# Turning angles moved from VectorE to GpSimd, with new orders on ScalarE and VectorE at five places

## The reference, cut to what matters

```python
def s5_ssm(u, a_re, a_im, log_dt, b_re, b_im, c_re, c_im, d_skip, glu_w, glu_b):
    lam = lax.complex(a_re, a_im)
    lam_bar = jnp.exp(lam * jnp.exp(log_dt)[:, None])
    b_bar = ((lam_bar - 1.0) / lam)[..., None] * b_mat
    bu = jnp.einsum('bsgh,gph->bsgp', ug, b_bar)
    _, states = lax.associative_scan(combine, (a_seq, bu), axis=1)
    y = jnp.real(jnp.einsum('bsgp,ghp->bsgh', states, c_mat))
...
def first_block(x, ...):
    for layer in range(DEPTH):
        h = rmsnorm(x, pre_norm[layer])
        y = even_mixer(h, ...) if layer % 2 == 0 else odd_mixer(h, ...)
        x = x + rmsnorm(y, post_norm[layer])
...
def second_block(x, ...):
    for layer in range(DEPTH):
        h = h + hybrid_mixer(rms_norm(h, norm1_g[layer]), ...)
        h = h + expert_choice_ffn(rms_norm(h, norm2_g[layer]), ...)
    return rms_norm(h, final_norm_g)
```

## Time and profile before

| | us |
|---|---|
| median of 3 runs | 1636.35 |
| lowest and highest | 1635.52, 1637.13 |
| profiled execution, own time | 1636.07 |
| its span in the trace | 1634.2 |

### The profile page before, as it was taken

How to read it: one execution, slowest core, us unless ns; L and a number is a source line. 1 busy time by engine, 2 the same in 40 slices (tenths; PEclk the granted TensorE clock), 3 DMA queues, 4 the chain that set the end, 5 groups by cost and what they waited for, 6 DMA issues and landing times.

```text
span 1634.2 us, 28359 instructions
## 1 busy us (share of the span) xinstructions
PE 1307.5 (80%) x12516; PEld 923.0 (56%) x12516; DVE 574.0 (35%) x873; ACT 453.5 (28%) x580; POOL 137.4 (8%) x169
## 2 busy tenths in 40 slices
PE   8999999999999987566666667999987556565665
PEld 6789889998989743223222234889843223232232
DVE  7993774765484520000000001584521001000001
ACT  5337654445554311001010012555311001010011
POOL 0220200000314000000000000304000000000000
PEclk9999999999999999988899897999999988899878
DMA  8334344545435899999999999335899999999997
GB/s 279 104 129 155 117 172 155 200 163 204 155 139 197 371 426 426 428 428 428 428 429 428 429 428 405 139 113 222 344 427 427 427 429 429 428 428 428 429 426 301
DMA packets 79503, 515.59 MB, mean 316 GB/s; under 512 B 6544, under 2 KB 6928, under 8 KB 54592
## 3 DMA queue, kind: packets, MB, share of 16 engines
q1 hardware_dynamic: 76000, 509.21, 76.4%
q0 software_dynamic: 912, 2.83, 0.5%
q10 hardware_dynamic: 2512, 2.36, 0.4%
HBM read 513.33 MB, written 1.05 MB: 315 GB/s over the span
## 4 chain that ended last, share of the span: by engine, by line
DMA 45%; PE 38%; DVE 11%; ACT 2%; issue 2%; SPq 1%; DVEq 0%; ACTq 0%
DMA board<-in_w_down 24%; DMA board<-in_w_gate 21%; PE dense L1750 8%; PE dense L1752 8%; PE dense L1751 8%; PE bank L2321 4%; PE bank L2351 2%; DVE ring_parts L1273 2%; DMA ring<-in_even_w_in 1%; DVE board L1556 1%; ACT ring_parts L883 1%; DVE board L1547 1%; PE dense L1773 1%; PE bank L2144 1%; PE bank L2291 1%
## 5 line engine op out<-in xcount | busy, mean ns | idle before, releaser
L2321 PE MATMUL bank<-ring,board 128*32 128x256 f32 x2688 | 207.4, 459 | 145.7 <-DMA ring<-in_w_up 82.5
L2321 PEld LDWEIGHTS bank<-ring,board 128*32 128x32 f32 x2688 | 90.4, 124 | 257.1 <-DMA ring<-in_w_up 104.2
L1107 ACT ACTIVATE board<-bank 128x256 f32<-128x256 f32 x32 | 12.3, 384 | 731.7 <-PE bank L2321 731.7
L1273 DVE TENSOR_TENSOR ring_parts<-ring,ring_parts 128x4096 fp32r<-128x4096 f32 (+1 forms) x43 | 181.6, 4228 | 88.6 <-ACT ring_parts L883 88.5
L1663 DVE TENSOR_TENSOR board<-board,bank 128x256 f32<-128x256 f32 x32 | 13.5, 421 | 553.3 <-ACT board L1107 553.3
L883 ACT ACTIVATE ring_parts<-ring 128x4096 fp32r<-128x4096 f32 (+1 forms) x47 | 161.5, 3438 | 123.7 <-DMA ring<-in_w_in 31.7
L1750 PE MATMUL dense<-board_parts,ring_parts 128*128 128x256 f32 x624 | 179.4, 288 | 0.5 <-DVE ring_parts L1273 0.5
L1752 PE MATMUL dense<-board_parts,ring_parts 128*128 128x256 f32 x624 | 176.6, 283 | 0.0
L2321 PE MATMUL bank<-board 128*32 128x256 f32 x1408 | 108.8, 461 | 65.4 <-DMA board<-in_w_up 40.7
L1750 PEld LDWEIGHTS dense<-board_parts,ring_parts 128*128 128x128 f32 x624 | 119.7, 192 | 1.9 <-issue 1.6
L1752 PEld LDWEIGHTS dense<-board_parts,ring_parts 128*128 128x128 f32 x624 | 119.6, 192 | 0.0
(11 more groups left out here) (354 smaller groups left out, 2057.3 us busy)
## 6 DMA issues: line engine op xcount, KB each, us to landing
ring<-in_w_gate SPq DMA_DIRECT2D x44, 2048.0 KB, 41.4
ring<-in_w_up SPq DMA_DIRECT2D x40, 2048.0 KB, 41.6
ring<-in_w_down SPq DMA_DIRECT2D x40, 2048.0 KB, 41.0
board<-in_w_up SPq DMA_DIRECT2D x24, 2048.0 KB, 41.0
board<-in_w_gate SPq DMA_DIRECT2D x20, 2048.0 KB, 40.5
board<-in_w_down SPq DMA_DIRECT2D x20, 2048.0 KB, 40.7
ring<-in_w_in SPq DMA_DIRECT2D x18, 2048.0 KB, 7.8
ring<-in_even_w_in SPq DMA_DIRECT2D x9, 2048.0 KB, 8.6
```

The lines of the kernel that those rows point to most:

```text
L1273: tt(lo, slot_of(u), hi.bitcast(F32), ALU.subtract).then_inc(lo_done, 1)
L2321: last = mm(o.rearrange("p (m b) -> p m b", b=2), xeT[:, 4 * (j // 2) + k, :], cols.rearrange("p (m r b) -> p r m b", r=2, b=2)[:, q % 2], ...
```

## The change

1. The angles of the state space part are made by GpSimd, in five instructions instead of VectorE's eight, behind the transfer of the C matrix and ahead of the turning of the queries; the rounding of sine and cosine is done in one instruction of 2048 columns each. `frac_ready` counts to 1 instead of 2. The two roundings' memory is a free piece of the working area.
2. ScalarE makes unit 2's high part behind the copy of unit 0's result (L899) instead of ahead of it and of three DMA issues.
3. VectorE makes the low parts of units 1 and 2 between the products and the differences of a round of B's powers. Each stood behind a round's differences before, and now has the next round's two products ahead of it as well.
4. Seam 1: VectorE's addition of the second tile goes ahead of the first tile's gain differences; the quarters of unit 15's low part go behind the second tile's gain.
5. Seam 2: one quarter of the low part of the second unit moves from ahead of the second tile's normalising to behind its gain.
6. At both ends of the experts ScalarE sums the squares of a tile by halves (`rms_halves`), the first as soon as its half of x is there.

```diff
@@ GpSimd
             gp.wait_ge(rest_in, 16)
+            gp.wait_ge(phi_ready, 1)
+            nearest = area(14336, "p (f n) -> p f n", f=2, n=SSM_TILES * SB)
+            own.link(g.tensor_tensor(cs[:, 1, :].rearrange("p (t b) -> p t b", t=SSM_TILES),
+                                     cn("block_start").unsqueeze(1).to_broadcast([P, SSM_TILES, SB]),
+                                     small[:, 0, :].unsqueeze(2).to_broadcast([P, SSM_TILES, SB]), ALU.mult))
+            own.link(g.tensor_scalar(cs[:, 0, :], cs[:, 1, :], 0.25, None, ALU.add))
+            own.link(g.tensor_scalar(nearest, cs, ROUND, None, ALU.add))
+            own.link(g.tensor_scalar(nearest, nearest, -ROUND, None, ALU.add))
+            g.tensor_tensor(cs, cs, nearest, ALU.subtract).then_inc(frac_ready, 1)
...
@@ ScalarE
             high_part(1)
-            high_part(2)
             act.dma_start(masks[:].rearrange("p l n -> p (l n)"), a["pair_masks"]).then_inc(masks_in, 16)
...
             act.wait_ge(unit_done, 1)
             s.activation(u_steps, DP[0][:].rearrange("p z (c b i) -> p (z c) i b", c=2, i=SL), ACT.Copy).then_inc(dense_out, 1)
+            high_part(2)
...
                 load_sqrt()
                 for i in range(NT):
-                    act.wait_ge(x_ready, 6 + 6 * l + 2 * (i + 1))
-                    rms(i, x[:, i, :])
+                    at = 6 + 6 * l + 2 * i
+                    rms_halves(i, x[:, i, :].rearrange("p (b n) -> p b n", b=2), (x_ready, at + 1), (x_ready, at + 2))
...
@@ VectorE
             for i in reversed(range(SL)):
                 times(z, sm(3), sm(4))
+                if i in (1, 2):
+                    low_part(3 - i)
                 z = pair(B_AT + 32 * i)
                 own.go(tt(z[:, 0], by_re[:, 0], by_im[:, 1], ALU.subtract))
                 own.link(tt(z[:, 1], by_re[:, 1], by_im[:, 0], ALU.add))
-                if i >= 2:
-                    low_part(4 - i)
...
             dve.wait_ge(rest_in, 16)
-            own.link(tt(turns(1), cn("block_start").unsqueeze(1).to_broadcast([P, SSM_TILES, SB]),
-                        sm(0).unsqueeze(2).to_broadcast([P, SSM_TILES, SB]), ALU.mult))
-            own.go(ts(cs[:, 0, :], cs[:, 1, :], 0.25, None, ALU.add))
...
-            tt(cs[:, 0, :], cs[:, 0, :], nearest[0], ALU.subtract).then_inc(frac_ready, 1)
...
@@ VectorE, seam 1
+            def norm_between(name):
+
+                dve.wait_ge(row_in, 16)
+                add_rows(0, 1)
...
+                normalise(0)
+                gain_rows(0, name)
+                add_rows(1, 1)
+                gain_low(0, x_lo)
...
+                normalise(1)
+                gain_rows(1, name)
+                low_part(SECOND[0], 0)
+                gain_low(1, x_lo)
+                for n in range(1, 4):
+                    low_part(SECOND[0], n)
...
@@ VectorE, seam 2
                 add_rows(i, 2)
-                for n in range(2):
+                for n in range(1 if i else 2):
                     low_part(FIRST2[0] + i, n)
...
-                gain_out(i, "n1_0", x_lo2)
-            for n in range(2, 4):
+                gain_rows(i, "n1_0")
+                gain_low(i, x_lo2)
+            for n in range(1, 4):
                 low_part(FIRST2[0] + 1, n)
```

More of the change, by code:

```diff
@@ L838, in sincos @@
             def sincos(c):
-                act.wait_ge(frac_ready, 2)
+                act.wait_ge(frac_ready, 1)
                 angle = cs[:, :, 4 * SB * c:4 * SB * (c + 1)]
@@ L1139, in normalise, with gain_out @@
                     ts(xs[:, i, half], x[:, i, half], rstd[:, i:i + 1], None, ALU.mult).then_inc(xs_ready, 1)
-            def gain_out(i, name, low=None):
+            def gain_out(i, name):
                 for half in range(2):
@@ L1146, in gain_out, with gain_rows, gain_low @@
                     g = vc(name)[:, 4 * half:4 * half + 4].unsqueeze(2).to_broadcast([P, 4, P])
-                    if low is not None:
-                        c = slice(4 * half, 4 * half + 4)
-                        tt(xs[:].rearrange("p i (c s) -> p c i s", c=DC)[:, c, i, :],
-                           WB[2 * i + half][:].rearrange("p (c s) -> p c s", c=4), g, ALU.mult).then_inc(gained, 1)
-                        continue
                     tt(xT[:, 4 * half:4 * half + 4, i * P:(i + 1) * P],
                        WB[2 * i + half][:].rearrange("p (c s) -> p c s", c=4), g, ALU.mult).then_inc(xT_ready, 1)
-                for half in range(2 if low is not None else 0):
+            def gain_rows(i, name):
+                for half in range(2):
+                    count["xt"] += 1
+                    dve.wait_ge(xt_ps, count["xt"])
+                    c = slice(4 * half, 4 * half + 4)
+                    tt(xs[:].rearrange("p i (c s) -> p c i s", c=DC)[:, c, i, :],
+                       WB[2 * i + half][:].rearrange("p (c s) -> p c s", c=4),
+                       vc(name)[:, c].unsqueeze(2).to_broadcast([P, 4, P]), ALU.mult).then_inc(gained, 1)
+            def gain_low(i, low):
+                for half in range(2):
                     count["hi"] += 1
@@ L1172, in add_rows @@
                     tt(x[:, i, half], x[:, i, half], xs[:, i, half], ALU.add).then_inc((sum_half, x_ready)[b], 1)
-            def norm_between(k, name):
-                dve.wait_ge(row_in, 16 * k)
-                for i in range(NT):
-                    add_rows(i, k)
-                    if i:
-                        low_part(SECOND[k - 1], 0)
-                    dve.wait_ge(x_ready, 2 * (k - 1) + i + 1)
-                    dve.wait_ge(sum_half, 2 * (k - 1) + i + 1)
-                    normalise(i)
-                    if i:
-                        low_part(SECOND[k - 1], 1)
-                    gain_out(i, name, x_lo if k == 1 else x_lo2)
-                low_part(SECOND[k - 1], 2)
-                low_part(SECOND[k - 1], 3)
+            def norm_between(name):
+                dve.wait_ge(row_in, 16)
+                add_rows(0, 1)
+                dve.wait_ge(x_ready, 1)
+                dve.wait_ge(sum_half, 1)
+                normalise(0)
+                gain_rows(0, name)
+                add_rows(1, 1)
+                gain_low(0, x_lo)
+                dve.wait_ge(x_ready, 2)
+                dve.wait_ge(sum_half, 2)
+                normalise(1)
[4 more added lines that the diff above has]
+                    low_part(SECOND[0], n)
             def sm(n):
@@ L1424, in _ @@
             low_part(14)
-            norm_between(1, "pre1")
+            norm_between("pre1")
             def pool(g):
```

9 lines of the change are left out of this document (removed).

## The result

The changed kernel takes **1648.0 us** (median of 6 runs, 1645.4 to 1651.0) against 1636.3 us for the kernel before in the same comparison: ratio 1.0068, 95% interval 1.0058 to 1.0078, some 11 us slower. I had predicted 1642.3 us. The direction was right, the size 5 us too small, and the time lies above my range. The profiled run of the changed kernel has 1646.55 us of its own and a span of 1644.4 us, 10.2 us longer than before.

The account below looks back on a forecast made before the run. Expert weight transfers bound the kernel, so dense-stage microseconds reach the end nearly whole. Opening +6.5, seam 1 +0.1, seam 2 -0.5, ends +0.1 make +6.2 us on 1636.07: 1642.3 us, range 1633.0 to 1645.5.

Parts of the forecast that it names:

- My first rival: Opening: GpSimd does not hold VectorE up, or starts only after B's powers; 1633.3 us, chance 0.22.
- the second: Rival, opening: only GpSimd's two two-operand instructions hold VectorE, 6.6 us, the one-input ones don't; 1637.6 us, chance 0.12.
- The price of the three scalar instructions: GpSimd's angles: addition 1.05 us, two roundings 2.1 each, 5.2 in all at the copy's rate; other end 12.0.
- Its length less 0.15 to 0.2: VectorE and GpSimd take turns; each instruction holds the other back by its length less 0.15 to 0.2 us.
- TensorE's clock: Rival, opening: clock falls after idling, 1644 us, or scalar instructions run at the two-operand rate, 1649; together 0.08.
- my own main case: Opening: GpSimd's five instructions stop VectorE 11.3 us, B's powers come at 52.4; 1639.5 to 1645 us, chance 0.55.
- The gains behind it: Opening, after B's powers: ScalarE's copies no longer late, -0.5 us; TensorE's 0.66 us wait for block sums goes.
- the opening: Stretch with units 1, 2 and the powers: 7.7 - 0.5 - 0.7 = +6.5 us.
- Seam 1: TensorE waits 0.35 us for gain differences, saves 0.2 to 0.3 at the second tile; sum +0.1 us.
- Seam 2: One quarter of a low part leaves the second tile's path, TensorE's 0.46 us wait ends; -0.5 us.
- Ends: Both ends of the experts, squares by halves: start 0.6 us earlier, cost 0.5 a tile; together +0.1 us.
- ScalarE's order: Opening: copy of unit 0's result ahead of unit 2's high part ends TensorE's 2.28 us wait before block products.

Follow-up runs that it names:

- angles_only: The kernel before with only the angles moved to GpSimd, no new order: 1646.5 us, ratio 1.0062.
- scalars_only: Changed kernel, angles back on VectorE, GpSimd's key rotation held back, plus three GpSimd scalar additions on memory nobody reads: 1640.7 us, ratio 1.0030 to the kernel before.
- filler: Changed kernel with 26 more useless products in front of TensorE's wait for B's powers: 1646.3 us, ratio 1.0064 to the kernel before.
- scalar_order: The kernel before with only unit 2's high part moved behind the copy of unit 0's result on ScalarE: 1637.6 us, ratio 1.0009.
- angles_back: Changed kernel with the angles' eight instructions back on VectorE, all new orders kept: 1635.4 us, ratio 0.9991 to the kernel before.
- angles_late: Changed kernel with GpSimd's angles waiting until VectorE has made C's powers: 1643.6 us, ratio 1.0044 to the kernel before.
- rounding_once: Changed kernel with GpSimd's two roundings written as one instruction with two additions: 1642.7 us, ratio 1.0046 to the kernel before.

## Why the prediction was right or wrong

- **The bound, and where the change works: right.** The angles alone decide (`angles_only`), the loss stands in one place, and from 90 us to the last dense row before the experts all is shifted by 9.2 to 10.9 us.
- **Start at 20.7 us, in VectorE's chain: right** (21.1).
- **That GpSimd's instructions hold VectorE: right**, the one-input ones too (`scalars_only`). My first rival, 0.22, and the second, 0.12, are out.
- **The price of the three scalar instructions: wrong, the first step that failed.** I took the copy's rate of the earlier trace rows, 5.2 us for all three, "as the form with one input". They take 2.77 + 5.38 + 5.38 = 13.5 us alone, even above my other end of 12.0, and hold VectorE 7.7 us. The two with two operands were sized well: held 1.73 and 4.39, by my sum 2.0 and 4.6. In all 13.8 instead of 11.3, **2.5 us**, and B's powers at 54.9 instead of 52.4. Alone this would have given 1644.8 us, inside my range; with the second step, below, it is 1646.6, outside it.
- **"Its length less 0.15 to 0.2" as the hold: wrong for the one-input form**, where it is length less 1.9 us. The two errors worked against each other; with the true lengths (1.9 + 13.5 + 4.5) and my rule I would have had about 19 us of holds. That the holds are only 2.5 us off is luck.
- **TensorE's clock: wrong, the second step.** I saw the rival and gave it, with the two-operand rate, 0.08, though my own main case contained idle stretches as long as those that I named in it. Here it takes 11.8 us from the first transposes to the first products behind them (54.98 to 66.76), 10.5 before (44.73 to 55.24), where my sum had 0.5 us less than before: **1.8 us**, and `filler` gives 1.7 back. A consequence of the main case is no rival to it and belongs in its sum.
- **The gains behind it: about right.** The wait for block sums is gone (-0.7), and the shift falls from 11.5 to 10.4 us by the outputs Y. With +6.5 predicted for the opening, +2.5 and +1.8 give 10.8, against 10.4.
- **Seam 1: +0.1 predicted, -0.1 measured** (entry shifted by 10.37, exit by 10.26 us); the wait foreseen at 0.35 us is the 0.20 at 248.09. **Seam 2: -0.5 predicted, -0.7 measured** (9.85 to 9.17). **Ends: +0.1 predicted**, -0.09 at the first and +0.17 at the last. ScalarE's square of a half takes 0.63 us (at 1636.45), where the whole took 1.06.
- **ScalarE's order**: its wait went, as said. But I priced it and VectorE's order as if they could be told apart, and `scalar_order` shows that alone it makes B's powers later.
- **Not in my sum**: 0.4 us gained between the seams, and 0.6 us lost near 500 us, where TensorE waits 0.95 us for VectorE (0.31 before), by the same turns of VectorE and GpSimd. In the trace of `angles_back` the waits at this place, 1.46 and 1.02 us, are larger than what either seam gave.

## What to carry to other kernels

Before work is moved to GpSimd to relieve VectorE, look at what VectorE does at the moment when GpSimd's operands land: if it is a chain of two-input instructions that somebody waits for, every GpSimd instruction that reads stops it, and the work isn't moved away: here VectorE got rid of 8.2 us and was held 13.8, in a worse place. Price each form from a row of that very form and size: a scalar instruction is not a copy. And where a change makes TensorE idle for some microseconds, put the lower clock behind it into the sum.

## What the runs showed of the hardware

- A scalar addition on GpSimd took 2.77 us for 1024 columns and 5.38 for 2048 where a copy of 1024 took 1.05 and a fill of 2048 1.9 (9.28 us for five). On VectorE an addition of 1024 took 0.83 (at 68.01 in the trace of before). The Trainium skill (GPSIMD Engine Reference, "4.1 Engine selection") has GpSimd near VectorE's rate with one input; for the copy that may do, for the scalar form it is out by a factor of three.
- Such an instruction keeps VectorE's two-input instructions out for its length less about 1.9 us (0.83 of 2.77, 3.44 of 5.38), one with two inputs nearly to its end (4.39 of 4.50). The 1.9 us are no constant of all forms: with two additions the last 2.75 of 7.0 us held nothing, and pieces of 512 columns held 0.3 to 0.4 us each. As an estimate from these rows, at 2.6 us and 3.4 us for 1000 columns, both ends are some 700 to 800 columns. Whether they are the writing of results was not tried.
- Fills on GpSimd held VectorE not at all, in 9.3 us.
- Either engine can be the one that waits, and it waits long where the other's instruction is long. In `angles_late` GpSimd's rounding at 74.06 took 7.69 instead of 5.38 us, since a low part was ahead of it until 76.5, and in `rounding_once` a low part of 4.42 us took 8.71, since the subtraction was.
